# A decoder kernel whose top-k rounds are dealt to other units, and one reload of x issued earlier

## The reference, cut to what matters

```python
for l in range(DEPTH):                       # DEPTH = 2
    h = rmsnorm(x, norm_mix[l]);  proj = h @ w_in[l]
    y_a = s5_mixer(u, ...)                   # state-space mixer
    y_b = dsa_attention(dq, dk, dv, iq, ik, iw, rel_bias)
    y_c = retention(rq, rk, rv, rg, ret_gn[l])
    x = x + concatenate([y_a, y_b, y_c]) @ w_out[l]
    h = rmsnorm(x, norm_ffn[l]);  gate, up = split(h @ w_ffn_in[l], 2)
    x = x + (silu(gate) * up) @ w_ffn_out[l]
return rmsnorm(x, norm_final)
# in dsa_attention, for each block of 128 queries:
    score = where(causal, score, NEG_INF);  _, sel = lax.top_k(score, 256)
    # softmax over the selected keys alone
```

## Time and profile before

| | |
|---|---|
| median of 3 runs | 2586.95 us (2584.3 to 2587.97) |
| profiled execution, its own time | 2584.79 us |
| its span, first to last instruction | 2582.9 us |
| PE busy | 2502.1 us, 97% of the span |
| DVE, ACT, POOL busy | 1373.8, 1134.7, 1326.1 us |
| granted TensorE clock, mean | 0.994 |

### The profile page before, as it was taken

How to read it: one execution, slowest core, us unless ns; L and a number is a source line. 1 busy time by engine, 2 the same in 40 slices (tenths; PEclk the granted TensorE clock), 3 DMA queues, 4 the chain that set the end, 5 groups by cost and what they waited for, 6 DMA issues and landing times.

```text
span 2582.9 us, 34756 instructions
## 1 busy us (share of the span) xinstructions
PE 2502.1 (97%) x13515; PEld 1987.8 (77%) x13515; DVE 1373.8 (53%) x2559; ACT 1134.7 (44%) x1726; POOL 1326.1 (51%) x818
## 2 busy tenths in 40 slices
PE   8988979999999999999999999999999999999999
PEld 6776757778777877788777887777887788888887
DVE  3789766987952226942421395579787312211112
ACT  5242355676545433324344422466755443322222
POOL 3432345464645664545555632554655457565655
PEclk9999999999999999999999999999999999999999
DMA  6241112232222353223322342222222225233342
GB/s 171 82 150 43 50 50 90 62 95 80 76 64 66 99 164 98 82 82 90 90 76 80 90 135 58 74 74 79 81 78 64 68 66 204 78 106 103 99 121 90
DMA packets 385666, 232.92 MB, mean 90 GB/s; under 512 B 29592, under 2 KB 371552, under 8 KB 383072
## 3 DMA queue, kind: packets, MB, share of 16 engines
q1 hardware_dynamic: 385136, 229.62, 29.9%
q10 hardware_dynamic: 368, 1.08, 0.1%
HBM read 213.88 MB, written 14.69 MB: 88 GB/s over the span
## 4 chain that ended last, share of the span: by engine, by line
PE 84%; DVE 11%; ACT 2%; issue 1%; POOL 1%; DMA 0%; ACTq 0%; SPq 0%; DVEq 0%; POOLq 0%
PE psum L1884 80%; PE psum L2214 2%; DVE scores L1436 2%; DVE top L1434 2%; POOL w_lo L774 1%; DVE xs L1250 0%; DVE scores L1418 0%; DVE search_i L1458 0%; POOL h_lo L782 0%; PE psum L2039 0%; ACT xs L1123 0%; DVE h_lo L1315 0%; PE psum L2318 0%; DVE scratch L1526 0%; POOL ssq L791 0%
## 5 line engine op out<-in xcount | busy, mean ns | idle before, releaser
L774 POOL TENSOR_TENSOR w_lo<-w_raw,w_hi 128x1024 fp32r<-128x1024 f32 (+2 forms) x408 | 905.9, 2221 | 1109.2 <-ACT w_hi L888 1109.0
L1884 PE MATMUL psum<-h_hi,w_hi 128*128 128x512 f32 x1984 | 793.1, 400 | 17.4 <-ACT h_hi L912 7.5
L888 ACT ACTIVATE w_hi<-w_raw 128x1024 fp32r<-128x1024 f32 (+2 forms) x408 | 397.3, 974 | 903.5 <-PE psum L1884 865.1
L1884 PE MATMUL psum<-h_lo,w_hi 128*128 128x512 f32 x1984 | 763.1, 391 | 0.9 <-POOL h_lo L782 0.9
L1884 PE MATMUL psum<-h_hi,w_lo 128*128 128x512 f32 x1984 | 514.6, 390 | 0.0
L1884 PEld LDWEIGHTS psum<-h_hi,w_hi 128*128 128x128 f32 x1984 | 373.4, 188 | 129.6 <-issue 39.5
L1884 PEld LDWEIGHTS psum<-h_lo,w_hi 128*128 128x128 f32 x1984 | 373.5, 188 | 78.3 <-issue 1.9
L1884 PEld LDWEIGHTS psum<-h_hi,w_lo 128*128 128x128 f32 x1984 | 373.5, 188 | 76.6
L1250 DVE TENSOR_TENSOR xs<-xs,psum 128x512 f32<-128x512 f32 x160 | 110.0, 687 | 333.7 <-PE psum L1884 322.8
L1884 PE MATMUL psum<-a_hi,w_hi 128*128 128x512 f32 x704 | 279.5, 397 | 6.5 <-DVE xs L1250 6.5
L1884 PE MATMUL psum<-a_lo,w_hi 128*128 128x512 f32 x704 | 274.6, 390 | 0.0
(11 more groups left out here) (333 smaller groups left out, 3061.6 us busy)
## 6 DMA issues: line engine op xcount, KB each, us to landing
w_raw<-in_w_ffn_in_dram SPq DMA_DIRECT2D x176, 512.0 KB, 3.7
w_raw<-in_w_ffn_out_dram SPq DMA_DIRECT2D x96, 384.0 KB, 3.1
w_raw<-in_w_in_dram SPq DMA_DIRECT2D x68, 512.0 KB, 3.7
w_raw<-in_w_out_dram SPq DMA_DIRECT2D x32, 512.0 KB, 3.6
x_half<-xs SPq DMA_DIRECT2D x8, 1024.0 KB, 6.3
xs<-x_half SPq DMA_DIRECT2D x8, 1024.0 KB, 7.2
w_raw<-in_w_ffn_out_dram SPq DMA_DIRECT2D x32, 256.0 KB, 2.6
out_dram<-mixed SPq DMA_DIRECT2D x8, 512.0 KB, 3.4
```

Of the source, the lines that this page charges most:

```text
L774: eng.tensor_tensor(w_lo(u, n), w_raw[:, u % 3, 0:n], w_hi[:, u % 2, 0:n].bitcast(F32), ALU.subtract).then_inc(sems["weights_ready"], 1)
L888: act(w_hi[:, u % 2, 0:n], w_raw[:, u % 3, 0:n], ACTF.Copy).then_inc(sems["hi_ready"], 1)
L1884: return eng.matmul(out_, lhsT, rhs, start=start, stop=stop, skip_group_check=True)
```

## The change

Rounds 3 to 31 of block 4 were spaced evenly over rows 2 to 21. Now rounds 3 to 19 are spaced over rows 2 to 12, none stands in rows 13 to 15, and rounds 20 to 31 are spaced over rows 16 to 22. This holds for both layers. Beside it, the four loads of `xa` are taken out of the woven side list of the mixout window (l = 0, h = 1), where they stood behind units 5 and 6, and put right behind its first unit, in front of the rest of the window.

```diff
-        side += spaced(rounds(4, 3), 2, 22) + spaced(rounds(7), 22, 55)
+        side += spaced(rounds(4, 3, 20), 2, 13) + spaced(rounds(4, 20), 16, 23) + spaced(rounds(7), 22, 55)
@@
     main = window("mixout", 0, 1)
     out += main[:1] + [("sums", None)]
-    side = [("rstd", None), ("diag",), ("spread", "fill")] + [("dma", "load_xa", n) for n in range(4)] + param_steps(1)[10:14]
-    out += weave(main[1:N_OUT], side)
+    side = [("rstd", None), ("diag",), ("spread", "fill")] + param_steps(1)[10:14]
+    out += [("dma", "load_xa", n) for n in range(4)] + weave(main[1:N_OUT], side)
```

## The result

The changed kernel takes **2593.89 us** (median of 6 runs, 2591.76 to 2597.83) against 2586.62 us of the kernel before (6 runs): ratio **1.0031**, with 95% between 1.002 and 1.0041. It is slower, by 7.3 us (5.2 to 10.6 by the interval), where +6.1 was forecast and 2593.0 said.

The account below looks back on a forecast made before the run. PE, busy 97% of the span, was taken as the bound, with 11.0 us of waits for evictions at stake. Rounds +7.4 and loads -1.3 gave +6.1 us on 2586.95, so 2593.0 us, range 2585 to 2598.

Parts of the forecast that it names:

- Rows 3 to 12: One extra round, hidden up to row 9; row 11's two for one cost 0.45 us, swallowed by the next wait.
- Rows 13 to 16: Four rounds fewer, 7.1 us less DVE work, bring only 1.2 us; the rest is DVE idle for ACT.
- Rows 17 to 22: Ten rounds for seven, 5.3 us more DVE work; PE ends 3.7 us behind a layer, 7.4 in both.
- the step that carries the sign: Row 20: retention 12 waits for ACT's square root, then two rounds for one; eviction 20 at 559.2 against 556.55.
- The holds by POOL: DVE's waits for POOL in rows 13 to 22: 7.0 us in the new order, 4.1 in the old.
- the walk: Row-by-row model, operations at measured length with waits for POOL; gives the old order's starts to within 0.2 us.
- The Trainium skill's rule: DVE instructions with two SBUF inputs and GpSimd ones reading SBUF exclude each other; without it unit 25 3.9 us early.
- The loads: At the seam, fillnorm waits for POOL's sum of squares, so starts 1.3 us earlier, not 5.5; PE's stall becomes 1.1.
- the bound: Output unit 4's weights, delayed by the early loads: 0.8 us of slack left, nothing taken, 1 us as upper bound.
- the sum: Whole kernel: +7.4 for the rounds and -1.3 for the loads, +6.1 us.

Follow-up runs that it names:

- after_pause: Changed kernel with counts of jobs 10 and later and their narrows three rows later, blocks and search finish moved accordingly; 2601.55 us, 1.0062 of the kernel before.
- late_as_before: Kernel before with units 3 to 15 dealt as in the changed kernel, 17 to 22 as before, three rounds moved to mixer output units; 2587.73 us, ratio 0.9999.
- reload_only: Kernel before with only the early loads of xa, rounds dealt as before; 2587.72 us, ratio 1.0002.
- reload_no_ssq: Kernel before with the early loads of xa, and the norm's first fill into scratch not waiting for POOL's sum of squares; 2584.2 us, ratio 0.9988.
- after_split_lo: Changed kernel with POOL's low-weight subtraction issued as two of 512 columns in first-half feed-forward windows; 2589.11 us, ratio 1.001 to the kernel before.
- before_split_lo: Kernel before with POOL's low-weight subtraction issued as two of 512 columns in first-half feed-forward windows; 2586.42 us, ratio 0.9998.

## Why the prediction was right

*Rows 3 to 12.* Eviction 11 came at 512.90, or 512.20 with the 0.70 off (forecast 512.2), and eviction 12 at 515.41 (515.4). Right.

*Rows 13 to 16.* DVE waited for ACT L1094 and L1151 as said. With 0.70 off, evictions 14, 15 and 16 came at 523.48, 525.44 and 531.53, forecast 523.3, 525.3 and 531.4. after_pause shows that ACT's chain of counts is the reason: without it, PE gains 6.3 us on the kernel before from unit 13 to unit 19, where the changed kernel gains 1.0.

*Rows 17 to 22.* Evictions 17, 19 and 20 came at 540.26, 548.70 and 559.44 against 540.1, 548.5 and 559.2. DVE's timeline in row 20, which answers to the L1598 of the earlier trace rows:

```profile
552.82 1.48 DVE L1598 TENSOR_TENSOR scratch<-scratch,gsum 128x1024 f32<-128x1024 f32 x1 [2.41 <-ACT gsum L1158]
554.34 2.21 DVE L1599 TENSOR_TENSOR scratch<-scratch,gn_row 128x1024 f32<-128x1024 f32 x1
...
560.14 0.69 DVE L1379 TENSOR_TENSOR tmp<-psum,tmp 128x512 f32<-128x512 f32 x1
```

L1598 started at 552.12 with 0.70 off, hardly later than before, but after 2.41 us of idle time: row 19's missing round left a hole that ACT's square root kept open, and the two rounds of row 20 stand behind it. Of the 2.9 us by which eviction 20 is late, 1.8 are the one round more in row 20 and 1.0 is L1599, which took 2.21 us where it took 1.23 before. That is the step that carries the sign. Unit 22 waited 2.58 us where 2.8 was said, the transposes 1.42 where 1.7 was. The loss is 3.9 us a layer instead of 3.7; late_as_before, which differs there and in three rounds done earlier, shows that it hangs on these rows.

*The holds by POOL.* In rows 13 to 22 they come to 7.0 us, the walk's number: five narrows (0.78, 1.04, 1.41, 1.26 and 1.26 us over the free 0.16), L1598 (0.26 over 1.22) and L1599 (0.99). The Trainium skill's rule (SBUF — State Buffer, "SBUF: two separate sides") was borne out by intervention as well: shorter POOL instructions, and nothing else, take back 3.1 of 3.9 us a layer in these rows. What waits is not told by size: block 4's rounds never waited (0.77 to 0.83 us for each of their two long instructions in these rows), and a scalar_tensor_tensor on two int32 columns did. The prediction gives 1.17 us as the most a narrow took before; the longest in these rows was 1.32 us, at 549.84, which changes nothing in the walk's sum.

*The loads.* Fillnorm was let go by POOL's sum, and PE's stall came to 1.13 us against 1.1 forecast; the seam gave 1.3 us (900 to 960), as forecast. Output unit 4 waited 0.21 us for its weights, where none was forecast and 1 was the bound; that moved its start by 0.4 us and its second matmul by 0.1 more, and a wait of 0.35 us at 902.86 that was gone in this trace gave 0.5 back. Unit 3's weights did not keep their place here: ACT got them at 922.96, with 4.7 off 2.1 us later than before, and PE didn't wait for them. In reload_only neither was late.

*What the sum missed.* The clock. Between the first rows and the last column, one stretch at the lower level stood in the trace of before (at 2207.4), two in the trace after (965.8 and 1819.2). The one at 965.8 took back 1.5 us, which is more than the reload brought. The one at 1819.2 replaced the wait at the transposes in layer two, so that it cost nothing more; the stretch at 2207.4 is absent after, and gives 1.4 back. The table adds up so: 7.9 for the rounds, -1.3 for the seam, +1.5 and -1.4 for the clock, 0.2 in small steps, 6.9 us from its first column to its last, where the medians have 7.3. The forecast of 6.1 was right in its steps, 0.5 low on the rounds, and had no term for the clock. That the clock's two terms cancel, +1.5 and -1.4, is luck of this trace, and so is part of how near 2593.0 came to 2593.89.

## What to carry to other kernels

Work taken out of a crowded stretch helps only where the engine isn't then waiting for another in the same stretch; so count the idle time that will appear, not the work that goes, and look at what stands behind the place where the work is put. Place movable work by the slack of each deadline (the eviction that the next unit waits for), in front of a step that waits for another engine's answer, where it fills the wait, and never behind that step with a deadline next, as rows 19 and 20 show. And when a wait is put down to one thing, look for the semaphore that would be next: at this seam it kept 4.2 of the 5.5 us of DVE's idle time.

## What the runs showed of the hardware

TensorE's granted clock fell from 1.00 (2.4 GHz) to 0.50 (1.2 GHz), mostly for 3.4 us at a time, in places that follow no edit clearly. These windows of the changed kernel are the stretch behind the seam with what stands around it, and the one in layer two behind the wait of 2.61 us before unit 22.

```profile
955.70:965.70 10.00, 8.55 (x40) 5.50 (x40) 7.20 (x10) 6.38 (x10) 6.52 (x5) 1.00 0.39 78
965.80:969.20 3.40, 3.40 (x9) 2.62 (x9) 1.56 (x3) 0.59 (x3) 3.40 (x2) 0.50 0.24 68
969.20:979.20 10.00, 10.00 (x45) 8.29 (x45) 0.00 (x0) 2.35 (x4) 3.09 (x2) 1.00 0.19 53
1809.20:1819.20 10.00, 7.39 (x33) 5.86 (x32) 9.05 (x15) 6.09 (x10) 6.92 (x4) 1.00 0.35 105
1819.20:1822.60 3.40, 3.40 (x9) 2.61 (x9) 3.26 (x8) 2.44 (x6) 1.80 (x2) 0.50 0.00 0
```

Ahead of the second TensorE stood 2.6 us. In front of the first PE was busy for 8.55 of 10 us, in waits of 1.1 us at most. The kernel before has 8.56 of 10 us at the same place, with a stall of 2.36 us ahead of it, and no fall:

```profile
953.00:963.00 10.00, 8.56 (x40) 5.75 (x40) 6.88 (x11) 6.42 (x11) 6.52 (x5) 1.00 0.26 55
```

Of the seven kernels with the early reload, five show such a stretch within 20 us behind the seam (the exceptions are reload_no_ssq and after_split_lo), of the five without it two show one at the seam (late_as_before at 951.5, before_split_lo at 951.9). These two fell as PE started again behind its stall (2.73 us in late_as_before), the five some 11 us after it. With one trace a kernel, this neither binds the fall to the edit nor clears it; what decides stays open, and with it how much of the seam's gain a kernel keeps. In the five the price is the same, 1.5 to 1.6 us. In the two it was nothing that stayed (900 to 978 in the table: -0.2 in both): PE ran slower, but a wait of 0.59 us for ACT's h_hi that stands there in the kernel before was gone.
